# Layer 2 of a four-layer decoder trunk: gates turned in 32x32 blocks by VectorE and moved through DRAM instead of transposed by TensorE

## The reference

```python
def sliding_window_attention(h, w_in, w_out, sinks, cos, sin):
    ...
    proj = h @ w_in
    q, k, v, g = jnp.split(proj, [SW_WIDTH, SW_WIDTH + nkv, SW_WIDTH + 2 * nkv], axis=-1)
    q = rope(q.reshape(B, S, SW_Q_HEADS, d), cos, sin) * (d ** -0.5)
    ...
    m = jnp.maximum(jnp.max(s, axis=-1, keepdims=True), sk)
    e = jnp.exp(s - m)
    p = e / (jnp.sum(e, axis=-1, keepdims=True) + jnp.exp(sk - m))
    o = jnp.einsum('bhgnqk,bnkhd->bqnhgd', p.astype(vv.dtype), vv, preferred_element_type=jnp.float32)
    o = o.reshape(B, S, SW_WIDTH) * jax.nn.silu(g.astype(jnp.float32))
    return o.astype(h.dtype) @ w_out
```

## Time and profile before

| | us |
|---|---|
| median of three runs | 1711.88 |
| lowest and highest | 1711.56 and 1712.52 |
| the profiled execution, its time | 1712.57 |
| the profiled execution, its span | 1710.8 |
| mean granted clock of TensorE | 0.999 |
| PE busy | 1699.6 |
| DVE busy | 1188.9 |
| ACT busy | 911.4 |

### The profile page before, as it was taken

One profiled execution on the slowest core, in us unless ns is written; L12 is line 12 of the kernel. 1 busy time (PEld: TensorE's weight loads), 2 busy tenths in 40 slices (PEclk: granted clock), 3 DMA queues, 4 the chain that ended last, 5 costly groups with the idle time before them and its releaser, 6 DMA issues.

```text
span 1710.8 us, 24445 instructions
## 1 busy us (share of the span) xinstructions
PE 1699.6 (99%) x7890; PEld 1417.7 (83%) x7890; DVE 1188.9 (69%) x1909; ACT 911.4 (53%) x1400; POOL 38.9 (2%) x99
## 2 busy tenths in 40 slices
PE   9999999999999999999999999999999999999998
PEld 7888888888888888888888888888888888888887
DVE  7767677775769888865656465656676676777756
ACT  7454555554656666655544545454554555455543
POOL 1000000000000000000000000000000000000000
PEclk9999999999999999999999999999999999999999
DMA  8768676766875555478998699966877686767673
GB/s 286 244 194 262 201 245 215 233 216 220 264 216 161 160 159 153 154 234 194 190 166 271 177 201 182 265 182 216 260 227 237 195 265 200 247 214 232 223 237 126
DMA packets 230035, 364.53 MB, mean 213 GB/s; under 512 B 14950, under 2 KB 80044, under 8 KB 229836
## 3 DMA queue, kind: packets, MB, share of 16 engines
q1 hardware_dynamic: 229536, 362.94, 73.5%
q0 software_dynamic: 48, 0.13, 0.1%
q10 hardware_dynamic: 380, 0.56, 0.1%
HBM read 335.79 MB, written 27.79 MB: 213 GB/s over the span
## 4 chain that ended last, share of the span: by engine, by line
PE 95%; DMA 2%; issue 1%; SPq 1%; DVE 1%; ACT 0%; DVEq 0%; POOLq 0%; POOL 0%; ACTq 0%
PE acc L1136 29%; PE acc L1137 29%; PE acc L1138 29%; PE tp L1102 1%; PE tp L1137 1%; PE tp L1136 1%; PE tp L1138 1%; DMA raw<-in_ml_w_in_dram 1%; PE sc L1137 1%; PE sc L1136 1%; PE sc L1138 1%; DMA xres<-in_x_dram 0%; DMA qs<-q_turning 0%; DMA q_turning<-scr 0%; PE sc L1162 0%
## 5 line engine op out<-in xcount | busy, mean ns | idle before, releaser
L2015 DVE TENSOR_TENSOR w_lo<-raw,w_hi 128x1024 fp32r<-128x1024 f32 x583 | 703.2, 1220 | 401.4 <-ACT w_hi L1074 399.0
L1074 ACT ACTIVATE w_hi<-raw 128x1024 fp32r<-128x1024 f32 x583 | 610.2, 1056 | 454.9 <-PE acc L1138 401.6
L1136 PE MATMUL acc<-w_hi,xt_hi 128*128 128x512 f32 x1824 | 715.3, 392 | 1.7 <-DVE w_lo L2015 1.0
L1138 PE MATMUL acc<-w_hi,xt_lo 128*128 128x512 f32 x1824 | 711.0, 390 | 0.0
L1137 PE MATMUL acc<-w_lo,xt_hi 128*128 128x512 f32 x1824 | 710.4, 389 | 0.0
L1138 PEld LDWEIGHTS acc<-w_hi,xt_lo 128*128 128x128 f32 x1824 | 342.4, 188 | 72.3
L1136 PEld LDWEIGHTS acc<-w_hi,xt_hi 128*128 128x128 f32 x1824 | 342.6, 188 | 70.3 <-DVE w_lo L2015 1.6
L1137 PEld LDWEIGHTS acc<-w_lo,xt_hi 128*128 128x128 f32 x1824 | 342.6, 188 | 67.3
L1136 PE MATMUL acc<-w_hi,ot_hi 128*128 128x512 f32 (+1 forms) x456 | 176.6, 387 | 0.0
L1138 PE MATMUL acc<-w_hi,ot_lo 128*128 128x512 f32 (+1 forms) x456 | 175.8, 386 | 0.0
L1137 PE MATMUL acc<-w_lo,ot_hi 128*128 128x512 f32 (+1 forms) x456 | 175.8, 385 | 0.0
(11 more groups left out here) (306 smaller groups left out, 1226.5 us busy)
## 6 DMA issues: line engine op xcount, KB each, us to landing
raw<-in_da_w_in_dram SPq DMA_DIRECT2D x255, 512.0 KB, 4.4
raw<-in_ml_w_in_dram SPq DMA_DIRECT2D x96, 512.0 KB, 5.7
raw<-in_sw_w_in_dram SPq DMA_DIRECT2D x72, 512.0 KB, 3.7
raw<-in_da_w_out_dram SPq DMA_DIRECT2D x64, 512.0 KB, 4.0
raw<-in_sw_w_out_dram SPq DMA_DIRECT2D x32, 512.0 KB, 3.7
raw<-in_ml_w_in_dram SPq DMA_DIRECT2D x64, 256.0 KB, 7.3
raw<-in_ml_w_out_dram SPq DMA_DIRECT2D x32, 512.0 KB, 3.9
qs<-q_turning SPq DMA_DIRECT2D x12, 512.0 KB, 6.9
```

The costliest lines, as they stand in the source:

```text
L1074: act.activation(w_hi[:, q:q + 2, :], raw[:, 2 * p:2 * p + 2, :], ACT.Copy).then_inc(hi_ready, 1)
L1136: pe.matmul(out_ap, k_hi, m_hi, start=start, stop=False)
L1138: return pe.matmul(out_ap, k_lo, m_hi, start=False, stop=stop)
L2015: dve.tensor_tensor(w_lo[:, two, :], raw[:, two, :], w_hi[:, q:q + 2, :].bitcast(F32), ALU.subtract).then_inc(lo_ready, 1)
```

## The change

PE no longer transposes gs in layer 2. In slot 26, behind the second scaling, DVE turns gs in 32x32 blocks into the first 1024 columns of `scr`. SP writes that to a new DRAM tensor `g_turning` in slot 30 (four DMAs) and reads it back in slot 31, in the output phase in slot 32, into `scr` from column 3 * 384 on. DVE multiplies both halves into `th` in slot 28 of the loop, now from `scr` and no longer from PSUM, and in slots 30 and 31 in the output phase. ACT's `ot_hi` moves to slots 29 and 29, in the output phase 31 and 32; DVE's `ot_lo` stays in slots 29 and 30 and moves to 31 and 32 in the output phase. Slot 28 of SP is later than slot 28 of DVE would suggest: SP walks eight pairs ahead of PE and DVE about four, so SP's slots 30 and 31 come ahead of DVE's slot 28. The order of the output projection stays. A new wait stands before the first row maxima of each group: the four writes must be in.

```diff
--- before
+++ after
@@ -71,4 +71,5 @@
           score=12, softmax=16, p_T=14, p_copy=18, pv=(17, 19, 21, 23), o_sum=(22, 24, 26, 28),
-          sink=(20, 24), den=(22, 25), g_tanh=19, gate=20, g_scale=(23, 26), g_T=(22, 24),
-          o_gate=(26, 28), o_hi=(27, 29), o_lo=(29, 30))
+          sink=(20, 24), den=(22, 25), g_tanh=19, gate=20, g_scale=(23, 26), g_turn=26,
+          g_write=30, g_read=31, g_read_last=32,
+          o_gate=(28, 28), o_gate_last=(30, 31), o_hi=(29, 29), o_hi_last=(31, 32), o_lo=(29, 30), o_lo_last=(31, 32))
 ML = dict(qk_evac=11, q_turn=12, q_write=17, q_read=19, qk_copy=19, score=(17, 18), decay=(18, 19), weigh=(21, 22),
@@ -80,4 +81,4 @@
 
-    "tp_0":      ((0, 0, 4), (0, 0, 1), (0, 6, 1), (2, 1, 0)),
-    "tp_1":      ((0, 0, 4), (0, 0, 1), (0, 6, 1), (3, 1, 0)),
+    "tp_0":      ((0, 0, 4), (0, 0, 1), (0, 5, 1), (2, 1, 0)),
+    "tp_1":      ((0, 0, 4), (0, 0, 1), (0, 5, 1), (3, 1, 0)),
     "sc_0":      ((0, 0, 0), (0, 3, 0), (0, 8, 0), (2, 2, 0)),
@@ -109,2 +110,6 @@
     "g_scaled":  ((0, 0, 0), (0, 0, 0), (0, 2, 0), (0, 0, 0)),
+    "g_turned":  ((0, 0, 0), (0, 0, 0), (0, 1, 0), (0, 0, 0)),
+    "g_written": ((0, 0, 0), (0, 0, 0), (0, 64, 0), (0, 0, 0)),
+    "g_moved":   ((0, 0, 0), (0, 0, 0), (0, 16, 0), (0, 0, 0)),
+    "o_gated":   ((0, 0, 0), (0, 0, 0), (0, 2, 0), (0, 0, 0)),
     "x_turned":  ((0, 0, 0), (0, 0, 4), (0, 0, 3), (0, 0, 4)),
@@ -451,2 +456,8 @@
 
+        g_dram = nc.dram_tensor("g_turning", (P, T * JW), F32, kind="Internal").ap()
+        g_rows = g_dram.rearrange("(j n) (t i r) -> n t j i r", j=4, t=T, i=4)
+        g_blocks = scr_flat[:, 0:T * JW].rearrange("p (t j n) -> p t j n", t=T, j=4)
+        g_landing = scr_flat[:, 3 * BLK:3 * BLK + T * JW]
+        g_landed = g_landing.rearrange("p (a k r) -> p k a r", k=4, r=32)
+
         def out_bank(l, n):
@@ -512,2 +523,7 @@
 
+        def sw_due(w, what, b):
+
+            last = w.last_due(SW[what + "_last"][b])
+            return last if last is not None else w.loop_due(SW[what][b])
+
         def scale_col(l, c2):
@@ -605,2 +621,10 @@
 
+            def move_g(w, l):
+
+                if (i := w.due(SW["g_write"])) is not None:
+                    write(g_rows, g_blocks, "g_turned", in_iter(l, "g_turned", i, 1), "g_written")
+                for read_at, due in ((SW["g_read"], w.loop_due), (SW["g_read_last"], w.last_due)):
+                    if (i := due(read_at)) is not None:
+                        read(g_landing, g_dram, "g_written", in_iter(l, "g_written", i, 64), "g_moved")
+
             def move_x(w):
@@ -624,2 +648,4 @@
                     move_p(w, w.l)
+                if w.kind == "sw":
+                    move_g(w, w.l)
                 move_x(w)
@@ -983,4 +1009,4 @@
                 for b in range(2):
-                    if (i := w.due(SW["o_hi"][b])) is not None:
-                        act.wait_ge(free[f"tp_{b}"], in_iter(l, f"tp_{b}", i, 6))
+                    if (i := sw_due(w, "o_hi", b)) is not None:
+                        act.wait_ge(sig["o_gated"], in_iter(l, "o_gated", i, b + 1))
                         act.activation(ot_hi[:, bass.ds(4 * i + 2 * b, 2), :], th_rows[:, 2 * b:2 * b + 2, :], ACT.Copy)\
@@ -1218,11 +1244,2 @@
                             turn(tp[b][:, P * c:P * c + P], scr[:, h, P * c:P * c + P], f"tp_{b}" if c == 2 else None)
-                for b in range(2):
-                    if (i := w.due(SW["g_T"][b])) is not None:
-
-                        pe.wait_ge(sig["g_scaled"], in_iter(l, "g_scaled", i, b + 1))
-                        fill_wait(f"tp_{b}", in_iter(l, f"tp_{b}", i, 5))
-                        for c in range(2):
-                            for t in range(T):
-                                turn(tp[b][:, S * c + P * t:S * c + P * t + P],
-                                     gs[:, t, P * (2 * b + c):P * (2 * b + c) + P], f"tp_{b}" if c + t == 2 else None)
 
@@ -1785,10 +1802,15 @@
                                 op.then_inc(sig["g_scaled"], 1)
+                if (i := w.due(SW["g_turn"])) is not None:
+                    dve.wait_ge(sig["g_scaled"], in_iter(l, "g_scaled", i, 2))
+                    dve.transpose(g_blocks.rearrange("p t j (k n) -> p t k j n", n=32),
+                                  gs[:].rearrange("p t (k j n) -> p t k j n", k=4, j=4)).then_inc(sig["g_turned"], 1)
                 for b in range(2):
                     rows_b = th_rows[:, 2 * b:2 * b + 2, :]
-                    if (i := w.due(SW["o_gate"][b])) is not None:
-                        dve.wait_ge(full[f"tp_{b}"], in_iter(l, f"tp_{b}", i, 6))
+                    if (i := sw_due(w, "o_gate", b)) is not None:
+                        dve.wait_ge(sig["g_moved"], in_iter(l, "g_moved", i, 16))
                         dve.wait_ge(free["sc_1"], in_iter(l, "sc_1", i, 2 + 2 * b))
                         own.wait()
-                        dve.tensor_tensor(th[:, b, :], tp[b][:], th[:, b, :], ALU.mult).then_inc(free[f"tp_{b}"], 1)
-                    if (i := w.due(SW["o_lo"][b])) is not None:
+                        o_half = in_blocks(rows_b)
+                        dve.tensor_tensor(o_half, g_landed[:, 2 * b:2 * b + 2], o_half, ALU.mult).then_inc(sig["o_gated"], 1)
+                    if (i := sw_due(w, "o_lo", b)) is not None:
                         dve.wait_ge(sig["t_hi"], in_iter(l, "t_hi", i, b + 1))
@@ -1801,2 +1823,4 @@
                             dve.wait_ge(sig["sink_set"], in_iter(l, "sink_set", i, 1))
+                            if not (isinstance(i, int) and i == 0):
+                                dve.wait_ge(sig["g_written"], in_iter(l, "g_written", i, 0))
                         row_maxima(l, i, h, h, 0, in_iter(l, "sc_0", i, h), mask_sw)
```

## The result

| | before | after |
|---|---|---|
| median of 22 runs each, us | 1711.91 (1711.08 to 1714.30) | 1714.69 (1711.39 to 1717.57) |
| ratio after/before, 95% interval | | 1.0014 (1.0008 to 1.0021) |
| a second measurement (11 runs; before 33) | 1712.46 | 1714.56; ratio 1.0015 (1.0006 to 1.0024) |
| profiled execution: time, span | 1712.57, 1710.8 | 1717.57, 1715.7 |

The forecast was -0.1 us. The interval of the ratio lies wholly above 1, so the 2.8 us are a real loss, though they are under the 3.4 us that the prediction took for the least that can be told apart. Lines after are 26 higher (L1209 is L1235), on DVE 17 to 24 (L1759 is L1776, L1792 is L1814, L1796 is L1818).

A forecast was written before the change was run, and what follows sets the result against it. TensorE, busy 1699.6 of 1710.8 us, was taken to bound the kernel. Transposes removed (-3.5), waits at first scores (+2.7) and in the output phase (+0.75) gave -0.1 us: 1711.8 us against a median of 1711.88, range 1709.5 to 1717.4.

The forecast's parts named there:

- Removed, -3.5 us: TensorE, layer 2: 32 transposes of gs gone, eight groups of four at 0.44 us each, -3.5 us, at most -3.8.
- Transpose on DVE, 0: DVE slot 26: the 1.25 us transpose delays p_lo, but TensorE's last pv keeps 0.5 us to spare; cost 0.
- The way through DRAM: Sync queue: read goes out 4.6 us after the first write and lands 5.6 us later; the queue itself costs 0.
- First scores, +2.7: Loop, slot 28: TensorE waits 0.5 us for q_split plus 0.4 for the landing before the first score, three times.
- 0.44 us plus a semaphore (0.05): First score: q_split's first half ends at 631.30, TensorE arrives at 630.86; with the semaphore it waits 0.5 us.
- Output phase, +0.75: Output phase: the read lands at 733.45, so TensorE waits 0.75 us for ot_lo before chunk pair 6; no second wait.
- The sum: Whole kernel: -3.5 + 2.7 + 0.75 = -0.1 us, so 1711.8 us, no change.
- Behind it stand only loads of raw ... cost 0: Sync queue: raw loads behind the read are issued four pairs before ACT needs them and land in 3.7 us; cost 0.
- term 4: Loop, moved gate multiplies: TensorE waits 0.9 us before the first score in three places, +2.7 us.
- step 3: Four writes and a read added on the sync queue: loads behind them are not delayed, cost 0; read lands in 5.6 us.
- The rival of the late read: Slot 28: DVE waits for a read landing in 6.5 us or more; at 7.2 us +6.3, 1718.2 us; chance 0.25.
- just hold: Emptying sc_0 for later scores: DVE and TensorE stand 0.54 us closer, 0.56 us of DVE idle time covers it; cost 0.

The follow-up runs named there:

- r_after: The changed kernel measured once more, unaltered, beside the follow-up kernels: +2.1 us against the kernel before, ratio 1.0015 (1.0006 to 1.0024).
- pool_gate: Changed kernel with the loop's two gate products on GpSimd instead of DVE, ot_hi in slots 29, 30, ot_lo in 30, 31: +3.2 us against before, ratio 1.0019.

## Why the prediction was wrong

1. **Removed, -3.5 us: right**, at its upper end: with all of them gone and nothing in their place, -3.4 measured and -3.1 in layer 2, where 3 x 0.22 of gap and spacing came back.
2. **Transpose on DVE, 0: right.** No wait at pv.
3. **The way through DRAM: right.** 4.9 us to the read (4.6), landing 4.6, 5.6, 6.1 and 5.3 (5.6); in r_after 4.0, 4.6, 6.0 and 5.3. The 3.2 us that the prediction works out from the Trainium skill would have been too short for every one; the section gives that figure for the path by way of GpSimd, and these reads are issued by SyncE.
4. **First scores, +2.7: too small, +4.4.** The failed term is "0.44 us plus a semaphore (0.05)". The lateness was nearly right: at the first place q_split's first half, begun at 579.45, is done at 580.15, and TensorE would have been there at 579.65, 0.50 us for 0.44. On top come 0.23 and not 0.05, since the start of the score follows that of q_split by 0.92 to 0.96 us in every kernel in which it waits for it, and 0.1 at the matmul behind it, for which I had nothing: 0.83 per place instead of 0.5, three times +1.0. The earlier trace rows could not show the 0.23: q_split was early there, and its distance to the score told nothing of the shortest one. The landing wait was 0, 0.66 and 1.07, mean 0.58 for 0.4: +0.5; in r_after only one of the three was late, and layer 2 came to +0.4. The last 0.2 of the 1.7 is not accounted for.
5. **Output phase, +0.75: right**, 0.7.
6. **The sum left out what lies outside layer 2.** Layer 2 came to +1.4 and +0.4; the rest of the two medians' differences, 1.4 and 1.7, is outside it. The profiled executions show 0.6 and 0.8 of that behind layer 2; the remainder is not located. "Behind it stand only loads of raw ... cost 0" was right in layer 2, and I had no term for the load-bound stretch of layer 3. So this step fails too, with its mechanism open.

The mechanism in layer 2 was thus right, and its size too small: TensorE waits where the prediction said, but loses 4.4 us there for 2.7. The forecast of 1711.8 us missed by what term 4 lacked and by what step 3 had put at nothing outside layer 2.

The rival of the late read held in small: one place in three in r_after, two in three in the first profile. The claim that the 0.56 us of idle time at 645.51 "just hold" was right: there is no wait for sc_0.

## What to carry to other kernels

A unit of work taken off the bounding engine is worth its time only if what replaces it ends before the next thing that this engine needs from the replacing one; here the replacement stood in DVE's only gapless stretch, and moving other, less urgent work (ot_lo, ot_hi) behind q_split gave the loop its whole gain back. Count a dependency that becomes critical by the distance measured in a place where it was already the last to come, not by the end of the producer's record. And time a change by layers, too: a good part of this miss lay outside the layer that was changed.

## What the runs showed of the hardware

- Where TensorE waits for an operand from DVE, its matmul starts 0.23 us after the end of DVE's record (0.93 after the start of a half of 0.70), and the next matmul follows after 0.21 instead of 0.12 us. Which part of the 0.23 is the semaphore and which the end of the write was not tried.
- GpSimd beside DVE: a DVE operation of 0.29 us took 1.37, one of 1.22 took up to 2.31. GpSimd's own product of 128x512 took 1.28 us at the shortest, with DVE idle for most of it, and up to 2.27 beside DVE (pool_gate).
- In every profile with 1 MB per iteration through DRAM in layer 2 the DMA throughput of a saturated stretch 300 us later is lower, 174 to 178 GB/s for 183 to 185 without. Why is open.
